# The first product level of a packed block inverse moved from TensorE to VectorE, with the later levels respaced

## The chip, the cores and the metric

One NeuronCore of a Trainium2 chip runs the kernel. The metric is the device time of one launch in microseconds. The time before is the median of three runs.

## The reference, cut to what matters

The program is one decoder layer for 256 prompt tokens and 8 x 8 sampled tokens: RWKV-7 mixing (16 heads of 64) beside retention (8 heads of 128), an output projection, and a mixture of 32 experts. Everything is float32. The change lies in the RWKV-7 part, whose state obeys, for each head and token,

```python
def _wkv_step(S, inp):
    r, w, k, v, kk, b = inp
    sa = jnp.einsum('bhvk,bhk->bhv', S, -kk)
    S = S * w[:, :, None, :] + sa[..., :, None] * b[:, :, None, :] + v[..., :, None] * k[:, :, None, :]
    y = jnp.einsum('bhvk,bhk->bhv', S, r)
    return S, y
```

The kernel doesn't step through the tokens. It takes chunks of 64 tokens, and within a chunk `sa` is the solution of a triangular system of 64 unknowns, so each chunk and head needs the inverse of a unit triangular 64x64 matrix.

## The kernel before

**Stages.** A loop over 8 pairs (`PAIRS`; a pair is two RWKV heads and one retention head) fills the first 850 us or so. Then come the output projection and the experts. The first pair is written out ahead of the loop, the other seven are its body.

**The order in a pair.** Each pair has 7 projection tiles (`k r v q kr vr g`), and each tile is 16 matmuls of 128x128 weights with 320 tokens. A float32 matmul is two passes of TensorE, so a tile is 32 passes. A tile is cut in 8 parts of 2 matmuls (4 passes, `L717`), and the table `PLAN` says behind which part each small step stands: the text of a tile is split at `|`, the first piece stands behind part 0. All engines go through the same table in order, each taking what it has to do for a step. So the four passes of a part are the unit in which the small steps are spaced. A name with `-` is a step of the pair before, `@q` stands for the evacuation of tile q.

**The packed inverse.** The four 64-token chunks of both heads are kept as 32x32 blocks, four chunks side by side. It begins with a level made by masks (`u0`): with `Ac` the packed triangle, `inner[k]` the mask of level k and `unit` the identity, VectorE forms `Vc = Ac * inner[0] + unit`, transposes it by 32x32 blocks to `Uc`, and spreads `Uc` to block-diagonal form `Ud`. It counts the semaphore `inverse` up behind each of the two. Each later level k doubles the size of the inverted blocks, in three steps on TensorE:

- `kN` (`L775`): a transpose of `Uc`, evacuated by ScalarE to `V2`. It waits for `Uc`.
- `iN` (`L785`): four small products with the mask product `Am[k-1] = Ac * inner[k]`, spread by VectorE to `Zd`. It waits for `Ud` and for the mask product.
- `jN` (`L794`): four small products of `V2` and `Zd`, which VectorE adds to `Uc` and then spreads to `Ud` again.

Levels 1 to 4 are of this form, and level 5 (`L797`) is half as large. A second inverse, for the sampled tokens, is made meanwhile by `us0`, `zs1` (`L767`), `ds1` (`L772`), `zs2`, `ds2`. GpSimd makes the mask products in the step `am`: two for the second inverse (`As`) once `g4` is evacuated, then four `Am` once ScalarE's `ac` (the packed `Ac`) is there. Each counts `lmk` up. `tv`, `tb`, `tk` (`L754`) and `ts` (`L758`) are transposes of values and keys, and `rs0` (`L832`, `L835`) reads the initial states of the sampled tokens. `zs1` to `ts` and `rs0` share the PSUM bank `SB`, in the order of `BANKS`: each waits until the one before is evacuated.

VectorE's operations are chained: each waits for the one before it.

## Time and profile before

| what | value |
|---|---|
| median of 3 runs | 1889.58 us (1888.24 to 1889.68) |
| the profiled execution: time, span | 1887.94 us, 1886.2 us |
| TensorE busy | 1553.1 us (82%) |
| VectorE busy | 624.1 us (33%) |
| ScalarE busy | 274.7 us (15%) |
| GpSimd busy | 63.9 us (3%) |
| period of the loop over pairs | 94.34 us |

TensorE's time is counted with the latency of each pass, so a share of 99% in a stretch still may hold short waits. The period is the distance between the starts of `k1` in two neighbouring pairs.

### The profile page before, as it was taken

How to read it: one execution, taken by the hardware profiler on the slowest of the kernel's cores; microseconds unless marked ns; L12 is line 12 of the kernel's file. 1: busy time of each engine (PE TensorE's matmuls, PEld its weight loads, DVE VectorE, ACT ScalarE, POOL GpSimd, SP SyncE). 2: the span in 40 equal slices, each digit the busy share in tenths (PEclk: the TensorE clock that was granted, in tenths of full speed). 3: DMA queues.
4: the chain of work that ended last, by engine and by line, in shares of the span. 5: the costliest groups of instructions: out<-in, count | busy, mean ns of one | idle time of the engine just before them, and what ended most of it. 6: DMA issues, size and time to landing. Idle time of an engine off the chain costs nothing.

```text
span 1886.2 us, 24655 instructions
## 1 busy us (share of the span) xinstructions
PE 1553.1 (82%) x8958; PEld 894.7 (47%) x8958; DVE 624.1 (33%) x1260; ACT 274.7 (15%) x592; POOL 63.9 (3%) x95
## 2 busy tenths in 40 slices
PE   7999999999999999999996675756757667576664
PEld 4676767676767676766662231222312223122111
DVE  6746565656565656420031010110102101020014
ACT  2222222222222222210012000000000000000002
POOL 1000000000000000000000000000000000000000
PEclk9999999999999999999998787878878788787878
DMA  7323232323232323175389999999999999999996
GB/s 285 113 92 110 93 110 91 110 91 110 93 110 91 109 94 110 68 274 237 134 362 428 428 428 428 429 428 428 429 428 428 428 428 428 428 428 428 429 407 252
DMA packets 71905, 510.35 MB, mean 271 GB/s; under 512 B 20497, under 2 KB 23697, under 8 KB 37809
## 3 DMA queue, kind: packets, MB, share of 16 engines
q1 hardware_dynamic: 71808, 509.60, 66.9%
q8 instruction: 29, 0.48, 0.1%
q14 instruction: 20, 0.16, 0.0%
q0 software_dynamic: 48, 0.12, 0.0%
HBM read 499.87 MB, written 9.82 MB: 270 GB/s over the span
## 4 chain that ended last, share of the span: by engine, by line
PE 57%; DMA 34%; DVE 5%; issue 1%; SPq 1%; ACT 1%; DVEq 0%; ACTq 0%
PE ps_PJ L717 23%; DMA arena<-w_up 22%; DMA arena<-w_down 12%; PE ps_C L1061 8%; PE ps_PJ L915 7%; DVE arena L1414 5%; SPq L556 1%; PE ps_C L1112 1%; PE ps_SB L1112 1%; PE ps_YB L1112 1%; PE ps_RT L890 1%; PE ps_C L785 1%; PE ps_RT L1112 1%; ACT arena L1144 1%; PE ps_SB L754 1%
## 5 line engine op out<-in xcount | busy, mean ns | idle before, releaser
L717 PE MATMUL ps_PJ<-arena 128*128 128x320 f32 x1792 | 539.0, 436 | 0.0
L1061 PE MATMUL ps_C<-arena 128*32 128x512 f32 x2048 | 284.9, 719 | 179.9 <-DMA arena<-w_gate 113.1
L717 PEld LDWEIGHTS ps_PJ<-arena 128*128 128x128 f32 x1792 | 323.3, 190 | 122.5 <-issue 20.7
L1414 DVE TENSOR_TENSOR arena<-arena,ps_PJ 128x512 f32<-128x512 f32 (+2 forms) x112 | 73.5, 656 | 613.1 <-PE ps_PJ L1015 493.4
L1061 PEld LDWEIGHTS ps_C<-arena 128*32 128x32 f32 x2048 | 79.4, 130 | 378.6 <-issue 376.2
L1414 DVE TENSOR_TENSOR arena<-arena 128x320 f32<-128x320 f32 (+11 forms) x310 | 161.6, 521 | 63.8 <-ACTq L418 25.6
L1144 ACT ACTIVATE arena<-ps_C 128x128 f32<-128x128 f32 (+3 forms) x68 | 27.4, 404 | 919.1 <-PE ps_C L1061 532.2
L915 PE MATMUL ps_PJ<-arena 128*128 128x320 f32 x512 | 142.5, 433 | 1.0 <-DVEq L418 1.0
L1144 ACT ACTIVATE arena<-arena 128x320 f32<-128x320 f32 (+11 forms) x206 | 97.8, 475 | 268.5 <-DVEq L418 88.1
L915 PEld LDWEIGHTS ps_PJ<-arena 128*128 128x128 f32 x512 | 95.5, 190 | 40.7 <-issue 4.0
L1414 DVE TENSOR_TENSOR arena<-ps_PJ,arena 128x512 f32<-128x512 f32 x32 | 22.1, 691 | 257.7 <-PE ps_PJ L1008 257.6
L1112 PE MATMUL ps_C<-arena 128*32 128x512 f32 x224 | 41.6, 823 | 79.6 <-DMA arena<-w_down 78.4
L1015 PE MATMUL ps_PJ<-arena 128*128 128x512 f32 (+1 forms) x192 | 96.2, 621 | 3.5 <-ACTq L418 3.3
L1008 PEld LDWEIGHTS ps_PJ<-arena 128*128 128x128 f32 x768 | 87.0, 192 | 12.6 <-issue 12.6
L1008 PE MATMUL ps_PJ<-arena 128*128 128x128 f32 x768 | 89.9, 277 | 0.0
L1959 POOL TENSOR_TENSOR arena<-arena 128x128 f32<-128x128 f32 (+2 forms) x72 | 57.8, 803 | 709.5 <-DVEq L418 377.4
L1414 DVE SCALAR_TENSOR_TENSOR arena<-arena 128x320 f32<-128x320 f32 (+4 forms) x144 | 67.8, 471 | 14.3 <-DVE arena L1414 9.4
L1414 DVE TENSOR_TENSOR arena<-ps_C,arena 128x384 f32<-128x384 f32 (+4 forms) x77 | 45.3, 588 | 60.4 <-PE ps_C L785 21.6
L1015 PEld LDWEIGHTS ps_PJ<-arena 128*128 128x128 f32 (+1 forms) x192 | 26.6, 170 | 72.5 <-DVEq L418 45.3
L1414 DVE RECIPROCAL arena<-arena 128x320 f32<-128x320 f32 (+1 forms) x29 | 54.5, 1881 | 6.0 <-ACTq L418 2.6
L1144 ACT ACTIVATE arena<-ps_SB 128x512 f32<-128x512 f32 (+4 forms) x80 | 36.4, 455 | 131.6 <-PE ps_SB L754 51.4
L1112 PEld LDWEIGHTS ps_C<-arena 128*32 128x32 f32 x224 | 7.0, 125 | 95.3 <-issue 95.3
(182 smaller groups left out, 1186.8 us busy)
## 6 DMA issues: line engine op xcount, KB each, us to landing
arena<-w_down SPq DMA_DIRECT2D x64, 2048.0 KB, 21.0
arena<-w_gate SPq DMA_DIRECT2D x61, 2048.0 KB, 20.6
arena<-w_up SPq DMA_DIRECT2D x61, 2048.0 KB, 20.3
arena<-win SPq DMA_DIRECT2D x59, 1024.0 KB, 4.8
arena<-w_out SPq DMA_DIRECT2D x16, 1024.0 KB, 6.9
arena<-w_gate SPq DMA_DIRECT2D x6, 1024.0 KB, 7.9
arena<-xT SPq DMA_DIRECT2D x8, 640.0 KB, 7.3
arena<-s_ret SPq DMA_DIRECT2D x8, 512.0 KB, 3.8
```

What stands on the lines that cost most here:

```text
L556: sp.dma_start(dst, src).then_inc(ex_in[s], 16)
L717: last = mm(pj(j)[:, 0:T], wt[j % NSLOT][:, kt, :], hT[:, kt, :], start=kt == 0, stop=kt == KT - 1)
L754: last = nc.tensor.transpose(b[:, c * P:(c + 1) * P], src[:, c, :], ident)
L785: last = mm(o, Am[:, k - 1, c, :] if k < INNER else A5[:, c, :], Ud[:, c, :, :] if k < INNER else Ud[:, c, 0:NB32:2, :], start=True, stop= ...
L915: last = mm(pj(m)[:, 0:T], w[:, i, :], yT[:, KORD[i], :], start=i == 0, stop=i == KT - 1)
L1008: last = mm(XB[b][:, k * P:(k + 1) * P], x1[:, t, kt * P:(kt + 1) * P], pick[:, t, :], start=t == 0, stop=t == 2)
L1015: mm(XB[b][0:nt, :], gT[:, t0:t0 + nt], yp[:, n * F:(n + 1) * F], start=True, stop=True).then_inc(x_full[b], 1)
L1061: last = mm((GB, UB)[u][h * CAP:(h + 1) * CAP, :], xg[:, kt, h * CAP:(h + 1) * CAP], w[h](k), start=kt == 0, stop=kt == KT - 1)
L1112: last = mm(DB[n][h * CAP:(h + 1) * CAP, :], hhT[:, 2 * k + j, h * CAP:(h + 1) * CAP], w[h][:, j, n * F:(n + 1) * F], start=k + j == 0, st ...
L1144: ins = nc.scalar.activation(*args, **kw)
L1414: ins = build(*args)
L1959: ins = nc.gpsimd.tensor_tensor(*args)
```

## The change

Level 1 is taken from TensorE. Step `u0` on VectorE now goes on behind `Vc`: it copies rows to their neighbours within groups of four partitions with two shuffles (`rows4`), multiplies and adds single columns and pairs of columns out of every group of four (`x1`, `v1`, `sx`, `pair4`), and adds the corrected `Am[0]` to `Vc` before the block transpose to `Uc`. The steps `k1`, `i1`, `j1` are gone with their places in the PSUM banks and their copies on ScalarE and VectorE. GpSimd makes `Am[0]` first, then the two `As`, then the other three `Am`, all behind the wait for `ac`. The second inverse's `zs1` waits for one mask product more. In `PLAN` the levels 2 to 5 are spread anew, and `rs0`, `tb`, `tk` and the rotary steps move.

```diff
-    "q": "@v ax am -va u0 | cv us0 | | k1 i1 | zs1 | j1 pd | ds1 | k2 i2",
-    "kr": "@q | rqa j2 zs2 | | rqb k3 i3 | ds2 | j3 | tv | k4 i4",
-    "vr": "@kr | rka j4 rs0 tb | tk | rkb k5 i5 -pr | ts vt | j5 rs1 | tkk -pw |",
+    "q": "@v ax am -va u0 | cv us0 | | k2 i2 | zs1 | j2 pd | ds1 |",
+    "kr": "@q | k3 i3 rqa | zs2 | j3 rqb | ds2 | k4 i4 | tv | j4 rs0",
+    "vr": "@kr | tb rka | k5 i5 | tk rkb -pr | ts vt | j5 rs1 | tkk -pw |",
...
+        rows4, pair4 = cut(3584, 128, c=NC), inv[:, 1536:1600].rearrange("p (g e) -> p g e", e=2)
...
                 elif s in ("zs1", "zs2"):
                     k = int(s[-1])
-                    pe.wait_ge(lmk, (INNER + 1) * p + k)
+                    pe.wait_ge(lmk, (INNER + 1) * p + 1 + k)
...
                 elif s[0] == "k":
-                    pe.wait_ge(inverse, 2 * (INNER * p + int(s[1])) - 1)
+                    pe.wait_ge(inverse, 2 * ((INNER - 1) * p + int(s[1]) - 1) - 1)
...
+            third_row = [i // 4 * 4 + 2 for i in range(32)]
+            second_row = [i // 4 * 4 + (1 if i % 4 == 0 else 2) for i in range(32)]
+
+            def by_four(x):
+
+                return x.rearrange("p c (g e) -> p (c g) e", e=4)
...
                     TT(Vc[:, :, :], Vc[:, :, :], unit[:, None, :].broadcast_to([P, NC, BK]), ALU.add)
+                    x1, v1, sx = by_four(Am[:, 0, :, :]), by_four(Vc), by_four(rows4)
+                    SHUF(rows4[:, :, :], Vc[:, :, :], third_row)
+                    dve.wait_ge(lmk, (INNER + 1) * p + 1)
+                    TT(pair4[:, :, 0:1], x1[:, :, 2:3], sx[:, :, 3:4], ALU.mult)
+                    TT(x1[:, :, 3:4], x1[:, :, 3:4], pair4[:, :, 0:1], ALU.add)
+                    SHUF(rows4[:, :, :], Am[:, 0, :, :], second_row)
+                    TT(pair4[:, :, :], sx[:, :, 2:4], v1[:, :, 1:2].broadcast_to([P, BK, 2]), ALU.mult)
+                    TT(x1[:, :, 2:4], x1[:, :, 2:4], pair4[:, :, :], ALU.add)
+                    TT(Vc[:, :, :], Vc[:, :, :], Am[:, 0, :, :], ALU.add)
                     TR(Uc.rearrange("p c j -> p (c j)"), Vc.rearrange("p c j -> p (c j)")).then_inc(inverse, 1)
                     spread(Ud, Uc).then_inc(inverse, 1)
...
                 if s == "am":
                     wait_freed(pool, "g4", p)
+                    pool.wait_ge(done("ac"), 2 * p + 1)
+                    TT(Am[:, 0, :, :], Ac[:, :, :], inner[1][:, None, :].broadcast_to([P, NC, BK]), ALU.mult).then_inc(lmk, 1)
                     for k in range(1, 3):
                         TT(As[:, k - 1, :], GM[:, NC, 0:P], lvlT[k], ALU.mult).then_inc(lmk, 1)
-                    pool.wait_ge(done("ac"), 2 * p + 1)
-                    for k in range(1, INNER):
+                    for k in range(2, INNER):
```

First place: VectorE around `u0`, in the loop's body, with the waits. Before, from the two products of `Vc`:

```order
L1414 TENSOR_TENSOR arena<-arena 128x128 [waits done_ac]
L1414 TENSOR_TENSOR arena<-arena 128x128 [waits vector_chain]
L1414 STREAM_TRANSPOSE arena<-arena 128x128 [waits vector_chain]
L1414 TENSOR_TENSOR arena<-arena 128x512 [waits vector_chain]
L1414 ISA [waits vector_chain]
L1414 COPY arena<-arena 128x1
```

After, in the same place:

```order
L1415 TENSOR_TENSOR arena<-arena 128x128 [waits done_ac]
L1415 TENSOR_TENSOR arena<-arena 128x128 [waits vector_chain]
L1415 STREAM_SHUFFLE arena<-arena 128x128 [waits vector_chain]
L1606 ISA [waits vector_chain]
L1415 TENSOR_TENSOR arena<-arena 128x32 [waits level_masked]
L1415 TENSOR_TENSOR arena<-arena 128x32 [waits vector_chain]
L1415 STREAM_SHUFFLE arena<-arena 128x128 [waits vector_chain]
L1415 TENSOR_TENSOR arena<-arena 128x64 [waits vector_chain]
L1415 TENSOR_TENSOR arena<-arena 128x32x2 [waits vector_chain]
L1415 TENSOR_TENSOR arena<-arena 128x128 [waits vector_chain]
L1415 STREAM_TRANSPOSE arena<-arena 128x128 [waits vector_chain]
L1415 TENSOR_TENSOR arena<-arena 128x512 [waits vector_chain]
```

Seven operations have come between `Vc` and the transpose that the first `kN` waits for, and one of them waits for GpSimd's first mask product.

Second place: TensorE from `j4` (four products of 32x128) to `tk`; `tb` is the first group of four 128x128 transposes behind `rs0` (the products of 24x128 and 16x128). Before:

```order
L794 MATMUL ps_C<-arena 32x128 x4
L832 MATMUL ps_SB<-arena 24x128 x8
L835 MATMUL ps_SB<-arena 16x128 x8
L754 MATMUL ps_SB<-arena 128x128 x4
L717 MATMUL ps_PJ<-arena 128x320 x2
L754 MATMUL ps_SB<-arena 128x128 x4
```

After, in the same place:

```order
L795 MATMUL ps_C<-arena 32x128 x4
L833 MATMUL ps_SB<-arena 24x128 x8
L836 MATMUL ps_SB<-arena 16x128 x8
L718 MATMUL ps_PJ<-arena 128x320 x4
L755 MATMUL ps_SB<-arena 128x128 x4
L718 MATMUL ps_PJ<-arena 128x320 x2
```

Two parts of projection (four matmuls) now stand between `rs0` and `tb`, which wait for one another through the bank `SB`.

Third place: GpSimd's loop body. Before:

```order
L1959 TENSOR_TENSOR arena<-arena 128x128 [waits free_SB]
L1959 TENSOR_TENSOR arena<-arena 128x128 [waits pool_chain]
L1976 ISA [waits pool_chain]
L1959 TENSOR_TENSOR arena<-arena 128x128 [waits done_ac]
L1959 TENSOR_TENSOR arena<-arena 128x128 [waits pool_chain] x3
L318 REGISTER_ALU [waits pool_chain]
```

After:

```order
L319 ISA
L1991 ISA [waits free_SB]
L1976 TENSOR_TENSOR arena<-arena 128x128 [waits done_ac]
L1976 TENSOR_TENSOR arena<-arena 128x128 [waits pool_chain] x5
L319 REGISTER_ALU [waits pool_chain]
```

The two products of the second inverse, which stood ahead of the wait for `ac`, now stand behind it, so that six operations follow `ac` in one go where there were four.

## Rows read from the trace of the kernel before

**Rows 1.** Busy time by stretch: us, PE, PEld, DVE, ACT, POOL, clock, DMA

```profile
0.00:94.00 94.00, 81.90 (x365) 52.28 (x366) 65.77 (x140) 24.05 (x48) 8.91 (x28) 1.00 0.54 198
...
658.00:752.00 94.00, 92.92 (x512) 65.87 (x504) 54.70 (x115) 23.39 (x56) 7.18 (x9) 1.00 0.29 101
...
1013.50:1020.00 6.50, 4.84 (x24) 1.38 (x28) 2.04 (x4) 0.00 (x0) 0.00 (x0) 0.50 1.03 439
```

**Rows 2.** Timeline of TensorE, from k1 of the fifth pair (start, duration in us, what)

```profile
450.61 0.27 PE L775 MATMUL ps_C<-arena 128*128 128x128 f32 x1
450.98 0.43 PE L785 MATMUL ps_C<-arena 128*32 128x128 f32 x8
451.34 1.34 PE L717 MATMUL ps_PJ<-arena 128*128 128x320 f32 x4
```

**Rows 3.** Timeline of TensorE, from k3 to j3 in the same pair

```profile
462.73 0.27 PE L775 MATMUL ps_C<-arena 128*128 128x128 f32 x1
...
463.29 1.34 PE L717 MATMUL ps_PJ<-arena 128*128 128x320 f32 x4
464.47 0.38 PE L772 MATMUL ps_SB<-arena 128*128 128x128 f32 x2
464.69 1.24 PE L717 MATMUL ps_PJ<-arena 128*128 128x320 f32 x4
465.86 0.43 PE L794 MATMUL ps_C<-arena 128*32 128x128 f32 x8
466.22 1.34 PE L717 MATMUL ps_PJ<-arena 128*128 128x320 f32 x4
```

**Rows 4.** Timeline of TensorE, from the second half of rs0 to tk

```profile
472.51 0.62 PE L835 MATMUL ps_SB<-arena 128*16 128x128 f32 x16
473.99 0.66 PE L754 MATMUL ps_SB<-arena 128*128 128x128 f32 x4 [0.86 <-ACTq L418]
474.48 1.24 PE L717 MATMUL ps_PJ<-arena 128*128 128x320 f32 x4
475.56 0.60 PE L754 MATMUL ps_SB<-arena 128*128 128x128 f32 x4
```

**Rows 5.** Timeline of VectorE in u0

```profile
448.64 0.85 DVE L1414 TENSOR_TENSOR arena<-arena 128x128 f32<-128x128 f32 x2 [0.24 <-DVE arena L1414]
449.53 0.32 DVE L1414 STREAM_TRANSPOSE arena<-arena 128x128 f32<-128x128 f32 x1
449.99 0.69 DVE L1414 TENSOR_TENSOR arena<-arena 128x512 f32<-128x512 f32 x1
```

**Rows 6.** Groups of instructions by form on VectorE (busy us, mean ns)

```profile
L1414 DVE TENSOR_TENSOR arena<-arena 128x32 f32<-128x32 f32 x19 | 3.7, 193 | 0.6
L1414 DVE TENSOR_TENSOR arena<-ps_RT,arena 128x64 f32<-128x64 f32 x8 | 1.8, 225 | 0.3
L1414 DVE TENSOR_TENSOR arena<-arena,ps_C 128x128 f32<-128x128 f32 x32 | 9.3, 290 | 25.5 <-PE ps_C L794 25.5
L1414 DVE STREAM_TRANSPOSE arena<-arena 128x128 f32<-128x128 f32 x34 | 10.7, 314 | 3.0
L1414 DVE STREAM_SHUFFLE arena<-arena 128x320 f32<-128x320 f32 x16 | 8.2, 515 | 0.2
L1414 DVE TENSOR_REDUCE arena<-arena 128x32 f32<-128x128 f32 x6 | 2.3, 376 | 0.3
L1414 DVE TENSOR_REDUCE arena<-arena 128x4 f32<-128x128 f32 x1 | 0.3, 287 | 0.0
```

**Rows 7.** Timeline of VectorE, the mask load of a shuffle

```profile
459.24 0.01 DVE L1414 LOAD_MASK_SELECT arena<-arena  x1 [0.15 <-DVE arena L1414]
```

**Rows 8.** Timeline of GpSimd in am

```profile
448.89 0.45 POOL L1959 TENSOR_TENSOR arena<-arena 128x128 f32<-128x128 f32 x1 [0.18 <-POOL arena L1959]
...
450.15 0.84 POOL L1959 TENSOR_TENSOR arena<-arena 128x128 f32<-128x128 f32 x1 [0.18 <-POOL arena L1959]
```

**Rows 9.** Timeline of TensorE, its longest wait inside the first pair

```profile
61.13 0.56 PE L747 MATMUL ps_SB<-arena 128*128 128x192 f32 x2 [1.54 <-DVEq L418]
```

More of the change, by code:

```diff
@@ L777, in step @@
                     k = int(s[1])
-                    pe.wait_ge(inverse, 2 * (INNER * p + k))
+                    pe.wait_ge(inverse, 2 * ((INNER - 1) * p + k - 1))
                     if k < INNER:
@@ L1244, in step @@
                     last.then_inc(done("ac"), 1)
-                elif s in ("k1", "k2", "k3", "k4"):
+                elif s in ("k2", "k3", "k4"):
                     wait_filled(act, s, p)
@@ L1601, in step @@
                     TR(Us, V[:, NC, :]).then_inc(done("us"), 1)
-                elif s in ("i1", "i2", "i3", "i4"):
+                elif s in ("i2", "i3", "i4"):
                     wait_filled(dve, s, p)
                     spread(Zd, bank(s)[:, 0:P].rearrange("p (b j) -> p b j", b=NB32)).then_inc(free(s), 1)
-                elif s in ("j1", "j2", "j3", "j4"):
+                elif s in ("j2", "j3", "j4"):
                     wait_filled(dve, s, p)
```

6 rows, old and new, of the table BANKS are left out of this document.

## The prediction

> **What bounds the kernel now.** I read the busy time by stretch first. In a stretch of 94 us inside the loop over pairs TensorE is busy for 92.92 us at a granted clock of 1.00, VectorE for 54.70, ScalarE for 23.39, GpSimd for 7.18, and the DMA engines for 0.29 of it [rows 1]. The reader is to see that TensorE sets the pace of the loop, and that nothing which frees the other engines helps unless TensorE waits for it. "Busy" counts the latency of each pass, so short waits hide in it. For them I went to TensorE's timeline and compared the starts of neighbouring groups. A part of projection (four passes) takes 1.08 us from start to start (474.48 to 475.56 [rows 4]); whatever a part or a small step takes beyond its plain price is a wait or a switch. From `k1` to `j5` of a pair two waits stand out. One is at `k1` and `i1`: 0.73 us from `k1` to the next projection (450.61 to 451.34 [rows 2]), where the same pair of steps takes 0.56 us at level 3 (462.73 to 463.29 [rows 3]). The other is at `tb`, of which the row says 0.86 us idle behind ScalarE [rows 4]. I then read VectorE and GpSimd around `u0`, since `k1` and `i1` wait for its results. The change touches the loop and its written-out first pair alone, in the same way 8 times. So all that follows is a balance for one pair, times 8.
>
> **What TensorE gets back.** First, a whole level is gone. Its price on TensorE, by level 3 [rows 3]: `k3` and `i3` 0.56 us; the four passes behind them take 1.18 us (463.29 to 464.47) and not 1.08, which is 0.10; the four ahead of `j3` take 1.17 (464.69 to 465.86), another 0.09; `j3` itself 0.36 (465.86 to 466.22); and by analogy 0.10 behind it. Together 1.21 us. Counting from `i2` in the new order and from `i1` in the old, everything up to `j5` is the same work but for this level.
>
> Second, `rs0` and `tb` are parted by two parts of projection. The 16 passes of `rs0`'s second half take 0.62 us with the latency of the last one, 0.27, so the last starts 0.35 us behind 472.51, at 472.86. A group behind such narrow products can start 0.20 us after the last of them (`i1`: 0.43 - 0.27 = 0.16 to its last pass, and 0.36 to the next group [rows 2]), that is at 473.06. It started at 473.99, a wait of 0.93 us [rows 4]. ScalarE's two copies that `tb` waits for now lie beside 2.16 us of projection, so the wait goes; if that cover were missing, the 0.93 would come back. The projection behind `rs0` pays the switch of 0.10 and `tb` loses some 0.05 of late weight loads. I count 0.89.
>
> The return is 1.21 + 0.89 = 2.10 us a pair. The rest of the respacing I cost at nothing: each of the steps keeps at least one part of projection, 1.08 us, between it and the step it waits for, where it had that before. The thinnest new cover is at `tv`: its bank waits for VectorE's `ds2`, which now stands behind `rqb`. By the old distances the evacuation comes just as `tv` is due, and I leave 0.0 to 0.1 for it.
>
> **What TensorE now waits for.** `k2` stands where `k1` stood, behind part 3 of `q`, but `Uc` comes later. Before, VectorE's transpose to `Uc` ended at 449.85 and the spread to `Ud` at 450.68 [rows 5]. `i1` followed 0.30 us behind `Ud`, at 450.98 [rows 2], the 0.17 us above being a wait for it. So there is no slack: `i2` comes later than `i1` came by all that `u0` has grown. Queued behind it on VectorE are `cv`, `us0` and the spread of `i2`, and on TensorE `zs1`, `j2` and `ds1` wait for them. They move by the same amount, so the delay is paid once.
>
> The growth, operation by operation, with the gap of 0.034 us between chained operations (two of 0.29 and the 0.23 explained below in 0.85 us [rows 5]):
> - two shuffles of 128 columns. Rows show 320 columns at 0.515 and a block transpose of 128 at 0.314 [rows 6]. From 320 to 128 at 1.04 ns a column (the products of 32 and 128 columns, 0.193 and 0.290, give 1.0) it is 0.315. The mask load takes 0.01 [rows 7], and I give 0.065 for it and its gap: 2 x 0.38 = 0.76.
> - two operations on 32 columns at 0.193 [rows 6]: 2 x 0.227 = 0.45.
> - two on 64 columns at 0.225 [rows 6]: 2 x 0.259 = 0.52.
> - one on 128 columns at 0.290 [rows 6]: 0.32.
> - the wait for the mask product: its computed count costs a register operation, some 0.10. The product itself is there, since GpSimd makes it first now, and its first product behind `ac` was over before the second began at 448.89 [rows 8].
>
> Together 2.15 us, if nothing disturbs it. But something does. Two operations of `u0` of 0.29 take 0.85 us together [rows 5]: 0.23 too much, from 448.97, when GpSimd's second product had just begun (448.89 [rows 8]). And GpSimd's product at 450.15 took 0.84 instead of 0.45, while VectorE's spread ran until 450.68. VectorE's operations with two inputs in SBUF and GpSimd's shut each other out. VectorE got going at 449.20, 0.31 us after GpSimd had begun. The block transpose at 449.53 wasn't held (0.32), so I take shuffles as free too. Now GpSimd has six operations in a row behind `ac` instead of four, 0.63 us apart (0.45 + 0.18), until about 452, and all of the new part of `u0` falls beside them. I lay the new operations against starts at 450.15, 450.78 and 451.41: the second of 32 columns waits 0.22 us, the first of 64 columns 0.02, and the last sum, behind a GpSimd product that itself had to wait, 0.13. That adds 0.37: 2.52 us.
>
> By the Trainium skill, page SBUF — State Buffer, section "SBUF: two separate sides", the pair of ports is an exclusive lock for the whole instruction. The exclusion is what the trace shows, but the row shows it free 0.31 us into an operation recorded at 0.45. By the page's rule each of the three waits would be 0.14 longer, and the growth 2.94.
>
> The narrow operations touch one or two columns out of every four, and nothing in `u0` before does that. The nearest row is the reduction that steps 32 columns at a time: 0.376 us for 128 elements against 0.287 for 128 in order [rows 6], 0.7 ns an element. For the 192 elements of the four operations that is 0.13 at most, and at least 0. I take 0.08. The same skill's page, section "Door 1: The DMA port swizzle", has lines of 16 bytes in SBUF and a penalty for each access that crosses into a new one, which speaks against this change: every group of four columns is a new line. It gives no figure for VectorE, so the sum stays.
>
> So `u0` grows by 2.60 us, with bounds of 2.15 (no exclusion, no stride) and 3.7 (each of the five products waits the full 0.31).
>
> **Sum.** 2.60 - 2.10 = +0.50 us a pair, 8 x 0.50 = +4.0 us. The profiled execution took 1887.94 us (span 1886.2, 1.7 around it), and would take 1891.9. The median of the runs, 1889.58, lies 1.6 above that execution, so the median after is 1893.6. The experts' stage moves as a whole.
>
> **Rivals.**
> - *The two sides cancel.* Without the exclusion the growth is 2.15 and the balance +0.05 a pair: +0.4 us, 1890.0. For it: the phase in which VectorE meets GpSimd may fall well. Against it: it happened in `u0` already [rows 5, 8].
> - *Faster.* The mechanism would be that `k2` doesn't wait, because the first results come by other slack. Then the 2.10 are free, 8 x 2.1 = 16.8 us: 1872.8. It decides from a growth under 1.6 us (8 x 0.5 = 4 us of gain). Against it: the seven operations' own durations alone, without gaps, are 2 x 0.315 + 2 x 0.193 + 2 x 0.225 + 0.29 = 1.76, and `i1` waited already.
> - *More waits.* If every product meets GpSimd, 3.7 - 2.1 = +1.6 a pair, 1902.4. By the page's rule above it is +0.84 a pair, 1896.3. A late `tv` adds at most 0.8 in all.
> - *The clock.* TensorE now stands still for some 2 us at `k2`. In the experts' stage the granted clock falls to 0.50 (1.2 GHz) for stretches such as 6.5 us [rows 1]. If a pair lost its clock for that long, every pass of 0.27 would take 0.54, and it would cost 3.2 us a pair, +26 beside the 4: 1919. Against it: TensorE stood still for 1.54 us ahead of 61.13 in the first pair [rows 9], and the granted clock of the first 94 us is 1.00 all the same [rows 1].
>
> **How the numbers follow.** The balance as argued, +0.2 to +1.0 us a pair (1891.2 to 1897.6): 0.62. The two sides cancel, from -0.2 to +0.2 a pair (1888.0 to 1891.2): 0.22. Faster: 0.05. More waits, beyond 1897.6: 0.08. The clock: 0.03. The likeliest gives 1893.6. A change of 0.2% (3.8 us) is what a measurement of this kernel can tell from none, and the forecast lies right at that line: 1893.4. Of the first case 0.36 lie above it and 0.26 below. So slower 0.36 + 0.08 + 0.03 = 0.47, same 0.26 + 0.22 = 0.48, faster 0.05. The range from 1889.3 to 1899.0 leaves out the faster case, the low end of the cancelling one, the clock, and the far end of more waits.
>
> **What the profile after would show.** Right: `k2`'s pass some 2 us later behind the last projection pass than `k1`'s was, `i2` 0.30 us behind the spread, `j5` (`L798`) 0.5 us later than now counted from the start of `u0`, no wait at `tb`, a period of 94.8 us, a clock of 1.00 throughout the loop. The new VectorE operations would stand at 0.315, 0.19, 0.19, 0.315, 0.23, 0.23 and 0.29, three of them lengthened beside GpSimd. Wrong: if the shuffles or the strided operations cost much more than columns times 1 ns, if `tv` or `j4` show a wait of their own, or if GpSimd's six products come so late that VectorE waits at the count.

## The result, and the profile after

The changed kernel takes 1900.61 us (median of 5 runs, 1897.04 to 1903.17), the kernel before 1889.68 (5 runs, 1888.24 to 1890.45). The ratio is 1.0059 with a 95% interval of 1.0048 to 1.0070: slower, by 11 us, where 4 were forecast, and above the range, which ended at 1899.0. The profiled execution took 1897.04 us, with a span of 1895.2, which is 9.0 longer than the span before.

On the page the engines' busy time has hardly moved:

```profile
PE 1553.3 (82%) x8822; PEld 896.4 (47%) x8822; DVE 627.5 (33%) x1308; ACT 272.7 (14%) x584; POOL 60.4 (3%) x95
```

The new VectorE work, seven operations of 2.2 us together in each pair, takes the place of the level's evacuations (627.5 us busy, 624.1 before). TensorE's 1553.3 us stand beside 1553.1 before, though a level is gone from it. Up to the end of the loop its busy time did fall, from 749.8 to 746.4 us. Behind the loop, where the work is the same and the mean clock is 0.85 in both, it is 807.0 us for 803.3, and the two differences cancel by chance. The sums of busy time don't show the loss; the waits and the clock do. The list of TensorE's waits says where it waits anew (line, what it waits for: us in total, times, longest):

```profile
PE ps_C L776 <- DVEq L419: 14.0, 8, 1.8
PE ps_C L786 <- DVEq L419: 5.7, 8, 0.8
```

Both come once a pair, at `k2` and at `i2`. TensorE's timeline in the fifth pair, where [rows 2] showed `k1` and `i1` before:

```profile
451.76 3.39 PE L718 MATMUL ps_PJ<-arena 128*128 128x320 f32 x12
456.89 0.33 PE L776 MATMUL ps_C<-arena 128*128 128x128 f32 x1 [1.74 <-DVEq L419]
457.91 0.43 PE L786 MATMUL ps_C<-arena 128*32 128x128 f32 x8 [0.69 <-DVEq L419]
458.27 1.34 PE L718 MATMUL ps_PJ<-arena 128*128 128x320 f32 x4
```

The twelve passes are issued in 12 x 0.27 = 3.24 us, so `k2` could have started at 455.00 and came 1.89 later. `i2` followed 1.02 behind it instead of 0.37, so another 0.65 us of standstill.

VectorE and GpSimd in the same pair, which answer to [rows 5] and [rows 8]:

```profile
453.02 0.85 DVE L1415 TENSOR_TENSOR arena<-arena 128x128 f32<-128x128 f32 x2 [0.24 <-DVE arena L1415]
453.92 0.30 DVE L1415 STREAM_SHUFFLE arena<-arena 128x128 f32<-128x128 f32 x1
454.35 0.71 DVE L1415 TENSOR_TENSOR arena<-arena 128x32 f32<-128x32 f32 x2
454.54 0.46 POOL L1976 TENSOR_TENSOR arena<-arena 128x128 f32<-128x128 f32 x1 [0.18 <-POOL arena L1976]
455.11 0.30 DVE L1415 STREAM_SHUFFLE arena<-arena 128x128 f32<-128x128 f32 x1
455.44 0.99 DVE L1415 TENSOR_TENSOR arena<-arena 128x64 f32<-128x64 f32 x3
455.81 0.47 POOL L1976 TENSOR_TENSOR arena<-arena 128x128 f32<-128x128 f32 x1 [0.18 <-POOL arena L1976]
456.46 0.32 DVE L1415 STREAM_TRANSPOSE arena<-arena 128x128 f32<-128x128 f32 x1
456.92 0.69 DVE L1415 TENSOR_TENSOR arena<-arena 128x512 f32<-128x512 f32 x1
```

The transpose starts 3.44 us behind the start of `u0`, where it was 0.89 before (448.64 to 449.53): the growth is 2.55 us.

So far the profile is as laid out. What was not is the granted clock. By stretches of 94 us (us, PE, PEld, DVE, ACT, POOL, clock, DMA), where [rows 1] have 1.00:

```profile
188.00:282.00 94.00, 91.44 (x491) 64.95 (x490) 54.43 (x120) 23.22 (x55) 6.78 (x9) 1.00 0.30 101
282.00:376.00 94.00, 91.42 (x482) 65.28 (x481) 53.42 (x116) 22.93 (x54) 6.80 (x9) 0.98 0.30 101
```

Three of the eight stretches have 0.98: the fourth, which is the second row here, the sixth and the eighth. Nearer, in the fourth pair, TensorE's timeline shows why:

```profile
360.66 0.33 PE L776 MATMUL ps_C<-arena 128*128 128x128 f32 x1 [1.74 <-DVEq L419]
361.69 0.66 PE L786 MATMUL ps_C<-arena 128*32 128x128 f32 x8 [0.70 <-DVEq L419]
362.27 2.50 PE L718 MATMUL ps_PJ<-arena 128*128 128x320 f32 x4
```

and the windows of 1 us there:

```profile
361.00:362.00 1.00, 0.31 (x8) 0.21 (x8) 0.57 (x3) 0.28 (x1) 0.00 (x0) 0.70 0.94 285
362.00:363.00 1.00, 1.00 (x10) 0.53 (x3) 0.79 (x4) 0.00 (x0) 0.00 (x0) 0.50 0.95 359
363.00:364.00 1.00, 1.00 (x3) 0.64 (x2) 0.78 (x2) 0.00 (x0) 0.00 (x0) 0.50 0.33 131
364.00:365.00 1.00, 1.00 (x5) 0.76 (x4) 0.17 (x1) 0.00 (x0) 0.00 (x0) 0.59 0.00 0
365.00:366.00 1.00, 1.00 (x5) 0.49 (x3) 0.00 (x0) 0.71 (x2) 0.00 (x0) 1.00 0.00 0
```

The reader is to see that TensorE comes out of the two standstills at half clock (1.2 GHz): the eight passes of `i2` take 0.66 us where the fifth pair has 0.43, and the four of projection 2.50 instead of 1.34. The windows lack 0.30, 0.50, 0.50 and 0.41 of their clock, which is 3.4 us at 0.50. The first of them puts the fall at 361.4, about 0.7 us behind the start of `k2` and still inside the second standstill. The first `k` and the next one are 10.4 us apart in this pair and 9.2 in the fifth, so a fall costs 1.2 us.

Read over the loop, the distance between the same transposes of neighbouring pairs (`tkk`) was 94.32 to 94.37 us before. After, it is 95.0 in four of the seven distances (one of them 95.17) and 96.2 in the three that hold a fall. That is the whole result of this execution: 8 x 0.65 = 5.2 us of plain lengthening, and 3 x 1.2 = 3.6 us of clock, 8.8 of the 9.0.

### The profile page after: what moved, and what is told of

Its sections match the earlier page's. It is cut to its first block, busy times and chain, and to the rows that moved or that the text cites. A ratio compares the mean times of both kernels' runs of the same rounds, so it can differ in the third digit from the quotient of the medians.

```text
span 1895.2 us, 24430 instructions
## 1 busy us (share of the span) xinstructions
PE 1553.3 (82%) x8822; PEld 896.4 (47%) x8822; DVE 627.5 (33%) x1308; ACT 272.7 (14%) x584; POOL 60.4 (3%) x95
## 4 chain that ended last, share of the span: by engine, by line
PE 54%; DMA 34%; DVE 8%; issue 2%; SPq 1%; ACT 0%; DVEq 0%; ACTq 0%
DMA arena<-w_up 22%; PE ps_PJ L718 21%; DMA arena<-w_down 12%; PE ps_C L1062 8%; DVE arena L1415 8%; PE ps_PJ L916 7%; SPq L557 1%; PE ps_C L1113 1%; PE ps_SB L1113 1%; PE ps_YB L1113 1%; PE ps_RT L891 1%; PE ps_RT L1113 1%; PE ps_C L786 1%; PE ps_SB L755 1%; PE ps_C L693 0%
## 5 line engine op out<-in xcount | busy, mean ns | idle before, releaser
L1415 DVE TENSOR_TENSOR arena<-arena 128x320 f32<-128x320 f32 (+14 forms) x342 | 168.7, 493 | 70.7 <-ACTq L419 35.8
L916 PEld LDWEIGHTS ps_PJ<-arena 128*128 128x128 f32 x512 | 95.5, 190 | 40.7 <-issue 4.0
L1016 PE MATMUL ps_PJ<-arena 128*128 128x512 f32 (+1 forms) x192 | 96.2, 621 | 3.5 <-ACTq L419 3.3
L1415 DVE TENSOR_TENSOR arena<-ps_C,arena 128x384 f32<-128x384 f32 (+4 forms) x69 | 39.7, 576 | 51.6 <-PE ps_C L786 23.8
```

Source lines behind the costliest of these rows:

```text
L916: last = mm(pj(m)[:, 0:T], w[:, i, :], yT[:, KORD[i], :], start=i == 0, stop=i == KT - 1)
L1016: mm(XB[b][0:nt, :], gT[:, t0:t0 + nt], yp[:, n * F:(n + 1) * F], start=True, stop=True).then_inc(x_full[b], 1)
L1415: ins = build(*args)
```

## The experiments

All times stand beside runs of the kernel before on the same chip: a median of 1888.76 us for the first four kernels (21 runs), 1887.72 for the next four (11 runs), 1887.88 for the last three (9 runs). "Before" is 1.0000. The ratio with its interval is the estimate on record and not the quotient of the two medians, from which it differs by up to 0.1%.

| kernel | median us (runs) | ratio, interval | period without a fall | pairs with a fall |
|---|---|---|---|---|
| changed | 1900.61 (5) | 1.0059, 1.0048 to 1.0070 | 95.0 | 3 |
| products ahead of `k2` | 1892.28 (11) | 1.0022, 1.0013 to 1.0031 | 95.0 | 0 |
| `k2` one part later | 1884.99 (11) | 0.9978, 0.9969 to 0.9987 | 93.9 | 0 |
| `k2` two parts later | 1874.61 (5) | 0.9925, 0.9912 to 0.9939 | 92.8 | 0 |
| without the new VectorE work | 1876.50 (5) | 0.9938, 0.9924 to 0.9951 | 92.9 | 0 |
| before, `tb` parted | 1880.56 (5) | 0.9962, 0.9949 to 0.9975 | 93.4 | 0 |
| GpSimd's old order | 1897.99 (5) | 1.0049, 1.0036 to 1.0062 | 94.8 | 5 |
| two parts later, GpSimd's old order | 1874.48 (5) | 0.9926, 0.9914 to 0.9939 | 92.7 | 0 |
| first shuffle three times | 1908.42 (6) | 1.0104, 1.0088 to 1.0121 | 95.5 | 2 |
| changed, again | 1900.86 (4) | 1.0059, 1.0044 to 1.0074 | 95.0 | 6 |
| shuffle three times, again | 1907.41 (1) | | 95.5 | 5 |
| shuffle three times, with products | 1899.64 (5) | 1.0058, 1.0044 to 1.0072 | 95.5 | 1, the first |

The last two columns are of the profiled execution of each. The theory: the excess over the forecast is the clock, which falls behind the standstill at `k2` and `i2`. The rival: it is made of plain waits that the balance left out.

**Products ahead of `k2`.** Eight products that nothing reads fill the standstill:

```diff
+                    if s == "k2":
+                        for _ in range(8):
+                            mm(b[:, 0:P], ident, ones, start=True, stop=True)
```

> The changed kernel with eight dummy matmuls of 128 columns on TensorE ahead of k2 (16 passes of 0.11 us, 1.75 us in all), which fill its wait of 1.9 us and delay nothing. Theory 1 (what went beyond the forecast is the clock: in some pairs TensorE's stand at k2 and i2 is followed by a granted clock of 0.5, 1.2 us each): the granted clock stays at 1.00 in the whole loop, every period is 95.0 us, and the time is that of before plus 8 x 0.66 = 5.3 us, 1895.0, with a spread like that of before (2 us instead of 6). Theory 2 (the longer periods come from the new VectorE work or from the new spacing): k2 to k3 stays at 10.4 us in some pairs, and the time stays at 1900.6.

TensorE's timeline, fifth pair, and the stretch of the loop that had 0.98:

```profile
453.02 1.95 PE L777 MATMUL ps_C<-arena 128*128 128x128 f32 x16
454.91 0.33 PE L779 MATMUL ps_C<-arena 128*128 128x128 f32 x1
455.97 0.43 PE L789 MATMUL ps_C<-arena 128*32 128x128 f32 x8 [0.73 <-DVEq L419]
```

```profile
282.00:376.00 94.00, 93.16 (x508) 66.98 (x507) 54.46 (x120) 23.20 (x55) 6.79 (x9) 1.00 0.29 101
```

`k2` still starts 5.12 us behind the group of twelve, which began at 449.79 (5.13 in the changed kernel), since VectorE is what it waits for. Added work on TensorE makes the kernel faster by 1.0059 - 1.0022 = 0.37%, some 7 us, no window in the loop is under 1.00, and every period is 95.0 (the first 95.15). The clock was worth about 7 us in the median, about six falls of 1.2 us, and 3.5 us above before are left. Over the loop the lengthening would be 8 x 0.65 = 5.2 us; the last `tkk` stands 4.8 us later than before's (769.96 for 765.18), and the experts' stage was 0.8 us shorter in this execution. The expected 1895.0 is counted from 1889.7; from the 1888.76 beside these runs it would be 1894.1, and 1.8 less was measured.

**`k2`, `i2` and all behind them later by one part, or by two.** With one part more ahead of `k2`:

```diff
-    "q": "@v ax am -va u0 | cv us0 | | k2 i2 | zs1 | j2 pd | ds1 |",
+    "q": "@v ax am -va u0 | cv us0 | | | k2 i2 | zs1 | j2 pd | ds1",
```

> The same with one part more only: 1.08 us of the wait is filled, 0.8 us stays at k2 and 0.8 at i2. Theory 1: 0.66 - 1.08 = -0.42 us a pair, -3.4 us against before, 1886.2, and no drop of the clock, since TensorE stands still for half as long. If the clock still drops in some pairs, 1.2 us for each of them come on top.

And two, with `ds1` at the start of the next tile:

```diff
-    "q": "@v ax am -va u0 | cv us0 | | k2 i2 | zs1 | j2 pd | ds1 |",
-    "kr": "@q | k3 i3 rqa | zs2 | j3 rqb | ds2 | k4 i4 | tv | j4 rs0",
+    "q": "@v ax am -va u0 | cv us0 | | | | k2 i2 | zs1 | j2 pd",
+    "kr": "@q ds1 | k3 i3 rqa | zs2 | j3 rqb | ds2 | k4 i4 | tv | j4 rs0",
```

> The changed kernel with k2 i2, zs1, j2, ds1 two parts later (k3 stays where it is), so that eight more passes of projection (2.16 us) lie beside the longer u0. The trace after has k2 due at 454.99 and starting at 456.89, i2 starting at 457.91. Theory 1: i2 starts at the same distance behind u0 as after, with 2.16 us more work done, so a pair takes 0.66 - 2.16 = -1.5 us against before, and no drop of the clock: 8 x -1.5 = -12 us, 1877.6. Theory 2 (the new work on VectorE costs wherever it stands, by holding other steps): less than half of that gain, above 1884.

`k2` and `i2` with one part more:

```profile
450.50 0.33 PE L776 MATMUL ps_C<-arena 128*128 128x128 f32 x1 [0.66 <-DVEq L419]
451.52 0.43 PE L786 MATMUL ps_C<-arena 128*32 128x128 f32 x8 [0.70 <-DVEq L419]
```

and with two:

```profile
446.32 0.27 PE L776 MATMUL ps_C<-arena 128*128 128x128 f32 x1
447.08 0.43 PE L786 MATMUL ps_C<-arena 128*32 128x128 f32 x8 [0.49 <-DVEq L419]
```

The wait at `k2` shrinks by the 1.08 us of the part (1.74 to 0.66) and is gone with the second. The periods are 93.9 and 92.8: 1.1 less for each part. In both the clock is 1.00 throughout the loop. The version with two parts is faster than both kernels, by 0.75% against before, and by 3 us more than expected. The loop itself gives what was expected (94.35 - 92.83 = 1.52 us a pair for 1.5). Of the 3 us, 0.8 is the base, since the expectation counts from 1889.6 and the runs beside this one stand at 1888.76; another 0.7 is the experts' stage, which was shorter by that much in the profiled execution. What it still pays is 0.49 us at `i2`, which stands right behind `k2`, while the spread to `Ud` ends 0.84 us behind the transpose.

**The new VectorE work left out.** The seven new operations of `u0` aren't made (so the first product level is missing from the inverse); the wait for GpSimd's first product is kept:

```diff
-                    SHUF(rows4[:, :, :], Vc[:, :, :], third_row)
                     dve.wait_ge(lmk, (INNER + 1) * p + 1)
-                    TT(pair4[:, :, 0:1], x1[:, :, 2:3], sx[:, :, 3:4], ALU.mult)
-                    TT(x1[:, :, 3:4], x1[:, :, 3:4], pair4[:, :, 0:1], ALU.add)
-                    SHUF(rows4[:, :, :], Am[:, 0, :, :], second_row)
-                    TT(pair4[:, :, :], sx[:, :, 2:4], v1[:, :, 1:2].broadcast_to([P, BK, 2]), ALU.mult)
-                    TT(x1[:, :, 2:4], x1[:, :, 2:4], pair4[:, :, :], ALU.add)
-                    TT(Vc[:, :, :], Vc[:, :, :], Am[:, 0, :, :], ALU.add)
```

> The changed kernel with the first product level left out altogether: the seven new operations of VectorE are gone and nothing is computed in their place. The level's return without its price. Theory 1: k2 and i2 stand as in the kernel before, the return of 2.09 us a pair less the 0.19 us of small waits that the trace after shows elsewhere is 1.9 us, 8 x -1.9 = -15 us, 1874.5, the clock at 1.00. Theory 2, if the spacing were at fault: k2 to k3 still 10.4 us in some pairs and a time above 1880.

```profile
445.69 0.43 PE L786 MATMUL ps_C<-arena 128*32 128x128 f32 x8 [0.30 <-POOLq L419]
446.05 1.34 PE L718 MATMUL ps_PJ<-arena 128*128 128x320 f32 x4
447.61 0.49 PE L768 MATMUL ps_SB<-arena 128*128 128x128 f32 x2 [0.21 <-DVEq L419]
```

The period falls to 92.9, so the seven operations cost 2.1 us a pair, and not their whole 2.55. Of the return of 2.10 only 1.47 shows (94.35 to 92.88). `i2` stands 0.20 us further behind `k2` than `i1` behind `k1` (0.57 for 0.37), since its mask product is now GpSimd's fourth behind `ac`, not the first, and that product is long in this trace:

```profile
444.66 0.93 POOL L1968 TENSOR_TENSOR arena<-arena 128x128 f32<-128x128 f32 x1 [0.18 <-POOL arena L1968]
```

It ends at 445.59, 0.10 us ahead of `i2`, while VectorE's spread had been over since 445.28. So GpSimd's new order makes a wait of its own at `i2` here, where `u0` is short. `zs1` comes 0.25 later (1.56 us behind the projection for 1.31 in the trace of before). The 0.18 that is left is taken up below.

**Before, with `tb` parted from `rs0` alone.** This is the second term of the return by itself. `tb` and, behind it, `tk` stand one part later:

```diff
-    "vr": "@kr | rka j4 rs0 tb | tk | rkb k5 i5 -pr | ts vt | j5 rs1 | tkk -pw |",
+    "vr": "@kr | rka j4 rs0 | tb | rkb k5 i5 -pr tk | ts vt | j5 rs1 | tkk -pw |",
```

> The kernel before with one thing of the change: a part of projection stands between rs0 and tb (rs0 | tb, and tk one part later). By the balance of the prediction the wait of 0.86 us at tb goes and a switch of 0.10 us between narrow and wide products comes back at most: -0.83 to -0.93 us a pair, -6.6 to -7.4 us in all, about 1882 on a chip where the kernel before takes 1888.8. Rival: the wait was only the visible end of ScalarE's copies and is met again one step on (tk or the projection behind it waits): 0 to -2 us.

```profile
469.05 0.62 PE L835 MATMUL ps_SB<-arena 128*16 128x128 f32 x16
469.60 1.34 PE L717 MATMUL ps_PJ<-arena 128*128 128x320 f32 x4
470.78 0.60 PE L754 MATMUL ps_SB<-arena 128*128 128x128 f32 x4
```

Against [rows 4] the projection starts 0.55 us behind the second half of `rs0`, and `tb` shows no wait. The period is 93.42 for 94.35: -0.93 us a pair, where the prediction has 0.89. The rival falls; the median gain is 0.38%, 7.2 us, for two steps moved in a table of the kernel before.

**GpSimd's order of before.** `As` first, then `Am`, in the changed kernel. The counts that `zs1`, `zs2` and `u0` wait for follow the order; their lines aren't shown:

```diff
-                    pool.wait_ge(done("ac"), 2 * p + 1)
-                    TT(Am[:, 0, :, :], Ac[:, :, :], inner[1][:, None, :].broadcast_to([P, NC, BK]), ALU.mult).then_inc(lmk, 1)
                     for k in range(1, 3):
                         TT(As[:, k - 1, :], GM[:, NC, 0:P], lvlT[k], ALU.mult).then_inc(lmk, 1)
-                    for k in range(2, INNER):
+                    pool.wait_ge(done("ac"), 2 * p + 1)
+                    for k in range(1, INNER):
```

> The changed kernel with GpSimd's order of before: the two mask products of the second inverse ahead of the wait for ac, then the four others. Fewer GpSimd products lie beside the new part of u0, so if the exclusion is worth 0.37 us a pair, some 0.15 to 0.3 us of it goes unless Am[0] itself is later. Theory (the clock): the standstill of TensorE gets shorter by the same amount, and any of the three falls of the granted clock that do not come are worth 1.2 us each. -1 to -5 us against the changed kernel, that is before + 6 to + 10 us. Rival (the clock has no part in it, the whole is a small lasting wait per pair): -1.2 to -2.4 us, every period the same.

```profile
457.88 0.33 PE L776 MATMUL ps_C<-arena 128*128 128x128 f32 x1 [1.54 <-DVEq L419]
455.52 0.70 DVE L1415 TENSOR_TENSOR arena<-arena 128x32 f32<-128x32 f32 x2
456.27 0.01 DVE L1415 LOAD_MASK_SELECT arena<-arena  x1
456.27 0.30 DVE L1415 STREAM_SHUFFLE arena<-arena 128x128 f32<-128x128 f32 x1
456.60 0.82 DVE L1415 TENSOR_TENSOR arena<-arena 128x64 f32<-128x64 f32 x3
```

GpSimd's last product now starts at 455.70 and is over by 456.15, so the three operations behind the second shuffle meet none and take 0.82 us instead of 0.99. The pair of narrow ones still meets one (0.70). The period without a fall is 94.8, 0.2 less. Yet the clock fell in five pairs instead of three, and this execution took 1898.28. A smaller standstill (12.7 us over the eight `k2` instead of 14.0) had more falls: how often the clock falls isn't set by the length alone. The median, 1.0049, can't be told from 1.0059 with certainty; the intervals overlap.

**Two parts later, with GpSimd's old order.** Both edits together:

> k2 and i2 two parts of projection later, as in the kernel with that change alone (before x 0.9925, 1874.6 us), and GpSimd's order of before as well. k2 does not wait there, so what u0 takes is hidden and GpSimd's order should be worth nothing: 1874.6, within 1.0. Rival: u0 still sets the pace somewhere behind (zs1, j2), then 1 to 2.5 us less.

```profile
446.43 0.42 PE L786 MATMUL ps_C<-arena 128*32 128x128 f32 x8 [0.31 <-DVEq L419]
```

The median is the same (0.9926 for 0.9925), as expected. The trace shows 0.31 us for 0.49 at `i2` and periods of 92.65 for 92.83, but 8 x 0.18 = 1.4 us, which the spread of the whole (1872.88 to 1876.45) swallows.

**The first shuffle three times.** More of the suspected cost; the shuffle's result is the same:

```diff
                     SHUF(rows4[:, :, :], Vc[:, :, :], third_row)
+                    SHUF(rows4[:, :, :], Vc[:, :, :], third_row)
+                    SHUF(rows4[:, :, :], Vc[:, :, :], third_row)
```

> The changed kernel with the first shuffle made three times over (its result is the same), which doubles the suspected cost: TensorE stands still for 0.66 to 0.70 us longer ahead of k2 in each pair, some 2.6 us where it was 1.9. Plain waits alone (rival): 8 x 0.68 = 5.4 us more than the changed kernel, before + 16.5, all periods alike at about 95.7. Theory (a standstill of this length lets the granted clock fall for 3.4 us, at 1.2 us a time): it now falls in all or nearly all pairs instead of 3 of 8 in the profiled run, periods of about 96.9, another 5 x 1.2 = 6 us, before + 20 to + 23.

```profile
457.51 0.33 PE L776 MATMUL ps_C<-arena 128*128 128x128 f32 x1 [2.22 <-DVEq L419]
```

The plain part came out lower than expected, 95.5 a period (the two shuffles cost 0.68 us, but the operations behind them met less of GpSimd: 0.65 and 0.86 us for 0.71 and 0.99, and the net is 0.48, so the standstill is longer by a fifth and not doubled). By plain waits alone that is 8 x 0.48 = 3.8 us, and a median near 1903 (1.0059 x 1887.7 + 3.8). The median is 1908.42, 20.7 above before, inside what the theory gave. But the theory had also said that the profiled execution would show a fall in all or nearly all pairs, and it shows two (periods of 97.87 and 96.76), in an execution of 1901.53 that was one of the two shortest of six (the others 1907.26 to 1911.83). That part of the expectation missed.

**The same two kernels again.**

> The changed kernel once more, on the same chip as the two beside it, to see whether the falls of the granted clock change from execution to execution. Theory (a standstill of 1.9 us and another of 0.8 us lets the clock fall sometimes, 1.2 us a time): loop periods are again 95.0 or 96.2 with nothing between, in other pairs than last time, and the span is 1895.2 plus or minus 1.2 us for each fall more or less than three. Rival (three particular pairs are slow for a reason of their own, by their data or their addresses): the fourth, sixth and eighth pair again.

The changed kernel's second profiled execution, of 1903.53 us, by stretches:

```profile
0.00:94.00 94.00, 79.50 (x339) 50.83 (x340) 65.39 (x143) 22.98 (x46) 8.21 (x28) 0.98 0.52 194
...
188.00:282.00 94.00, 91.44 (x476) 65.02 (x475) 52.72 (x117) 23.11 (x55) 6.78 (x9) 0.96 0.29 101
...
470.00:564.00 94.00, 91.42 (x492) 64.98 (x491) 54.49 (x120) 23.16 (x55) 6.79 (x9) 1.00 0.29 101
```

The stretch with 0.96 lies in a period of 97.67: there the clock stayed low twice as long (0.04 of the clock of these 94 us is missing, where a single fall takes 0.02), and it cost 2.7 us. Six pairs have a fall, one of them double; in the first execution it was three. The last `tkk` of the loop starts 5.1 us later than in the first (779.49 for 774.35), which is four falls more at 1.28, the double one counted as two. They lie in pairs 1 to 5 and 7, and the sixth and the eighth pair, which fell the first time, have none. The rival, three particular pairs, is out.

> The changed kernel with the first shuffle made three times, once more: its profiled execution had two pairs with falls and took 1901.5, while its median was 1908.4 and its longest 1911.8. Theory: its period without a fall is 95.5 again, and what the span has beyond 1896.7 (1899.7 less the 3.7 that the two slow pairs had too much) is 1.2 to 2.4 us for each pair in which the clock falls; an execution of 1908 would show six to eight such pairs. Rival (the spread is in the experts' stage): the loop is the same in all executions.

```profile
94.00:188.00 94.00, 91.09 (x473) 64.47 (x472) 48.60 (x113) 22.89 (x54) 6.76 (x9) 0.96 0.30 102
...
376.00:470.00 94.00, 90.94 (x491) 64.62 (x490) 55.51 (x125) 22.73 (x54) 6.76 (x9) 1.00 0.28 101
```

This execution took 1907.41 us; falls in five pairs, two of them double, so seven units where the first execution of the same kernel had three. The loop's last `tkk` is at 783.11 us instead of 777.72: 5.4 of the 5.8 us between the spans lie in the loop, four units at 1.35. The expected six to eight pairs weren't met (five), but in units of 1.2 to 1.4 us the sum holds, and the rival, a spread of the experts' stage, falls. (The expectation's 1896.7 is a slip: 1899.7 less 3.7 is 1896.0.)

**The shuffle three times, and products ahead of `k2`.** Both edits as above.

> The shuffle made three times, and eight products that nothing reads ahead of k2, as in the kernel with these products alone. The plain wait stays: 95.5 us a period. Theory (all that lies above it is the clock): no fall in the loop, all periods 95.5, a median of 1.2 x 8 = about 9 us above before (1896.5 to 1898 where before takes 1888.5), and a spread of under 3 us over the runs. Rival (the extra work on VectorE itself costs more than it seems): 1905 or more, as without the eight products.

```profile
0.00:94.00 94.00, 80.82 (x351) 52.45 (x352) 65.38 (x147) 22.73 (x45) 8.13 (x28) 0.98 0.53 194
94.00:188.00 94.00, 92.71 (x503) 66.51 (x500) 50.46 (x117) 22.88 (x54) 6.77 (x9) 1.00 0.29 102
```

All periods are 95.5 (the first 95.67), as without the products, and no clock falls but once in the first pair, behind waits of 0.98 and 0.55 us. The median goes from 1908.42 to 1899.64 and the spread from 11.4 us to 2.4. So most of the 9 us between the two are the clock. The expected 1896.5 to 1898 was missed by 1.6 to 3: the first pair's fall is 1.2 of it, and the experts' stage of the profiled execution was 2.5 us longer than before's (from the last `tkk` to the end 1123.5 for 1121.0), which no run here explains.

## Why the prediction was wrong, point by point

**What TensorE gets back: right.** From `i2` to `j5` it is 27.14 us after, and from `i1` to `j5` 29.23 before: 2.09 for 2.10. The second term alone was measured as 0.93 for 0.89, which leaves 1.16 for the level's 1.21. `tv` and `j4` show no wait, and neither does `tb`:

```profile
476.08 0.62 PE L836 MATMUL ps_SB<-arena 128*16 128x128 f32 x16
476.63 2.42 PE L718 MATMUL ps_PJ<-arena 128*128 128x320 f32 x8
478.89 0.60 PE L755 MATMUL ps_SB<-arena 128*128 128x128 f32 x4
```

**What TensorE waits for: right, with terms that were off in both directions.** The growth of `u0` is 2.55 for 2.60. The two shuffles with their mask loads cost 0.68 for 0.76, since the mask load (0.01) lies beside the shuffle's start and 128 columns take 0.30. The wait for the count costs 0.10 as taken. The operation of 32 columns that met no GpSimd product takes 0.215 us for the 0.193 of unit step, and the one of 64 columns 0.226 for 0.225: the stride costs 0.04 or so and not 0.08. The exclusion costs more than laid out: the second operation of 32 columns took 0.46 us instead of 0.215, the first of 64 columns 0.27 for 0.23, the sum of 128 0.43 for 0.29, together 0.43 for 0.37. The places were the three foreseen.

The first of these also decides between the row and the page. It began at 454.60, 0.06 us behind the GpSimd product of 454.54, which lasted until 455.00. It was over at 455.06, so its own 0.215 began at about 454.85, 0.31 into the product, as in [rows 5, 8]. By the rule of the Trainium skill, page SBUF — State Buffer, section "SBUF: two separate sides", that the lock is held for the whole instruction, it would have ended at 455.21. The trace disagrees by 0.15 us; the measurement decides.

`i2` 0.29 us behind the spread (457.62 to 457.91), `k2` 1.89 us late, `j5` 0.47 us later than before when counted from the start of `u0`, where 0.5 was written: all as laid out.

**"The rest of the respacing I cost at nothing": off by 0.18 us a pair.** The plain period is 95.0, not 94.8. Growth less return is 2.55 - 2.09 = 0.46 us, and the period grew by 0.65. Of the rest, 0.08 lies at `ms`: its weight load waits longer for VectorE, and the group takes 0.62 us from its start to the next one where it took 0.54:

```profile
502.13 0.30 PEld L887 LDWEIGHTS ps_RT<-arena 128*128 128x128 f32 x2 [0.32 <-DVEq L419]
```

The other 0.11 us lies at `g4` (`L748`), half a tile ahead of `u0`. Its first weight load stands idle for 0.40 us, and the one of before for 0.29:

```profile
537.73 0.30 PEld L748 LDWEIGHTS ps_SB<-arena 128*128 128x128 f32 x2 [0.40 <-issue]
```

In both kernels it comes 0.2 us behind a VectorE operation (which ends at 537.56 here, at 532.53 before). Why VectorE is later there isn't shown. The kernel without the new VectorE work has both, 0.14 us together, so they come with the level's absence or the new spacing, and not with the seven operations. By this term the whole would be 1893.6 + 1.4 = 1895, inside the range.

**The rival "the clock": this is the step that failed.** It was seen, given the price of a 6.5 us stretch (3.2 us a pair, in all pairs), and then given a chance of 0.03 because one standstill of 1.54 us in the first pair had left the clock at 1.00. Both halves were wrong. Its size: the fall lasts 3.4 us, of which the passes lose 1.2, and comes in three to six pairs of eight, so +4 to +9 us and not +26. Its chance: it leaned on a wait that isn't like the one at `k2`. The standstill in the first pair is a single one of 1.54 us, ahead of `g4` products in a row. All thirteen traces of this case have it, at 1.53 to 1.55 us, and the clock is 1.00 behind it in each, so it was no lucky draw; it was the wrong place to look. At `k2` there are 1.89 us, one narrow pass, and 0.65 more. In the two executions of the changed kernel a fall followed 9 times out of 16. Nor is the length of the longer standstill what parts the two places: with GpSimd's old order TensorE stands idle ahead of `k2` for 1.54 us too, with 0.70 behind it, and the clock fell in five pairs of eight. Whether it is the second standstill or the work around them that makes the difference, no run here tells apart. The kernel with 0.66 and 0.70 us of wait at `k2` and `i2` had no fall in 8 pairs, and neither had the changed kernel with products in the gap; with the longer standstill and products it was one in 8.

By the Trainium skill, page TensorE: Matmul & The Clock Gate, section "What's actually happening", the hardware watches activity on a clock of its own that no kernel resets, so that one kernel measures differently from run to run. The trace agrees as far as it goes: the clock of the same program fell in pairs 4, 6 and 8 in one execution, and in pairs 1 to 5 and 7 in the next. The falls began 0.67 to 0.75 us behind the start of `k2` in the one and 0.49 to 2.32 us in the other, though the standstills of all pairs but the first are alike to 0.02 us.

**"More waits"** at +0.84 to +1.6 a pair didn't come (the first of these leaves out the prediction's own 0.08 for the stride; with it, it is +0.92); the range's upper end of 1899.0, made from it, was overrun by 1.6 us by the clock. The likeliest case alone would have been near: with the clock held up by products the ratio is 1.0022, which is 1893.8 us on the scale of 1889.68, where 1893.6 was forecast. So close a hit would have been in part luck, since the periods alone give 1889.68 + 5.2 = 1894.9.

**"Faster"** was priced at 16.8 us for a `k2` that doesn't wait. The schedule that makes this so (two parts later) gains 14.2. Of the return of 2.10 us a pair this schedule keeps 1.52; 0.49 is still waited for at `i2`. What was missing was cover for `u0`.

## What to carry to other kernels

When a chain on another engine grows, move what waits for it back by as many parts of the main work as the growth is long, before judging the change: here the change with 2.55 us of new VectorE work a pair loses 11 us with the consumer left in place and gains 14 with it two parts later. A standstill of TensorE in a loop has two prices, the wait itself and a clock that may fall with it. A place where the clock held says little about another place with other work around it, however alike the waits are, so compare what stands ahead and behind, and count the places and executions. A spread over the runs that is several times that of the kernel before (6.1 us for 2.2 here) is itself a sign of it.

## What the runs showed of the hardware

- The granted clock fell to 0.50 for 3.4 us at a pair of standstills of 1.9 and 0.65 us with one pass between. In the changed kernel's two executions the fall began 0.5 to 2.3 us behind the start of that pass, in six of nine inside the second standstill, and each cost 1.2 to 1.4 us. Once in the second execution, and three times with a longer standstill, it stayed low twice as long.
- How often it falls changes between executions of one program: 3 and 6 pairs of 8, and 2 and 5 with 0.5 us more of standstill; with 0.16 us less it was 5. It also fell once behind waits of 0.98 and 0.55 us, in the first pair, with products ahead of them.
- A single standstill of 1.54 us in the first pair left the clock at 1.00 in all thirteen traces.
- Eight products that nothing reads, 1.9 us of them, left the start of `k2` where it was and kept the clock up in 15 pairs of 16: 7 us faster in one kernel, 9 in another.
- A shuffle of 128 float32 columns takes 0.30 us, and its mask load nothing beside it. Products on one column out of four take 0.215 us for 32 columns.
- A VectorE operation with two inputs in SBUF that came 0.06 us behind the start of a GpSimd product of 0.46 us got going 0.31 us into it.
